# Weights at other distances from the rows they meet, and down slots sorted by row length, in a two-block transformer kernel

## What is computed

```python
def swiglu(x, w_gate, w_up, w_down):                       # D_FF = 2816
    return (silu(x @ w_gate) * (x @ w_up)) @ w_down

def first_block(x, ...):
    for l in range(2):
        h = h + 0.5 * swiglu(rmsnorm(h, ffn1_norm[l]), ...)      # feed-forward parts 1 and 3
        z = rmsnorm(h, mix_norm[l]) @ w_in[l]                    # queries, keys, values, pool, three gates
        branches = stack([mla(z), diff_attention(z), pool(z)])   # each @ w_branch
        h = h + sum(sigmoid(z_gate) * branches) @ w_out[l]
        h = h + 0.5 * swiglu(rmsnorm(h, ffn2_norm[l]), ...)      # feed-forward parts 2 and 4
    return rmsnorm(h, final_norm)

def second_block(x, ...):
    proj = rms_norm(x) @ even_w_in      # even layer: stick-breaking attention and an S5 mixer
    x = x + concatenate([o_a, o_b]) @ even_w_out
    proj = rms_norm(x) @ odd_w_in       # odd layer: gated linear attention
    return x + (o * silu(z)) @ odd_w_out
```

## Time and profile before

| | |
|---|---|
| Median of three runs | 1491.08 us (1490.85 to 1492.25) |
| Profiled execution, its own time | 1489.85 us |
| Its span, first to last instruction | 1487.9 us |
| TensorE busy | 1477.5 us (99%), 9684 matmuls |
| VectorE, ScalarE, GpSimd busy | 1161.2 us (78%), 793.4 us (53%), 39.4 us (3%) |
| Weights and inputs read | 258.61 MB, 175 GB/s over the span |

### The profile page before, as it was taken

The page is one execution under the profiler, slowest core; times in us unless marked ns, Lnnn a source line. Parts: engine busy times, 40 slices in busy tenths (PEclk is TensorE's granted clock), DMA queues, the critical chain, the costliest instruction groups (busy, mean ns, idle before and its releaser), DMA issues.

```text
span 1487.9 us, 23067 instructions
## 1 busy us (share of the span) xinstructions
PE 1477.5 (99%) x9684; PEld 1318.9 (89%) x9684; DVE 1161.2 (78%) x1534; ACT 793.4 (53%) x995; POOL 39.4 (3%) x41
## 2 busy tenths in 40 slices
PE   9999999999999999999999999999999999999999
PEld 8888898888988888888889878799999999989978
DVE  7987777687798865988658677879998799766844
ACT  6444455565454443544436566455545645675653
POOL 0000001210000000000001020000000000000000
PEclk9999999999999999999999999999999999999999
DMA  8555545444455545555554544455554454335531
GB/s 287 203 193 198 173 173 184 158 143 169 166 191 191 192 176 198 188 184 194 183 202 139 192 152 160 151 213 206 193 197 177 154 184 145 142 106 188 178 139 57
DMA packets 38967, 261.15 MB, mean 176 GB/s; under 512 B 4688, under 2 KB 5584, under 8 KB 9168
## 3 DMA queue, kind: packets, MB, share of 16 engines
q1 hardware_dynamic: 38000, 258.62, 49.4%
q10 hardware_dynamic: 864, 1.05, 0.2%
HBM read 258.61 MB, written 1.05 MB: 175 GB/s over the span
## 4 chain that ended last, share of the span: by engine, by line
PE 91%; DVE 7%; ACT 1%; issue 1%; DMA 0%; ACTq 0%
PE ps L285 20%; PE ps L222 13%; PE ps L224 13%; PE ps L223 13%; PE ps L292 11%; PE ps L771 8%; PE ps L773 4%; DVE w_low L207 3%; PE ps L310 1%; PE ps L1513 1%; PE ps L312 1%; DVE scratch L2216 1%; PE ps L1504 0%; DMA w_raw<-in_weights 0%; PE ps L1486 0%
## 5 line engine op out<-in xcount | busy, mean ns | idle before, releaser
L207 DVE TENSOR_TENSOR w_low<-w_raw,w_high 128x2048 fp32r<-128x2048 f32 (+2 forms) x244 | 551.6, 2262 | 152.4 <-ACT w_high L201 150.8
L201 ACT ACTIVATE w_high<-w_raw 128x2048 fp32r<-128x2048 f32 (+2 forms) x244 | 459.7, 1885 | 378.7 <-PE ps L292 171.0
L285 PE MATMUL ps<-x,w_high 128*128 128x512 f32 x1328 | 317.1, 391 | 0.0
L285 PEld LDWEIGHTS ps<-x,w_high 128*128 128x128 f32 x1328 | 243.9, 188 | 47.5
L771 PE MATMUL ps<-ffn_hid,w_high 128*128 128x512 f32 x528 | 183.2, 390 | 0.0
L292 PEld LDWEIGHTS ps<-x,w_low 128*128 128x128 f32 x1328 | 170.3, 191 | 6.4
L292 PE MATMUL ps<-x,w_low 128*128 128x256 f32 x1328 | 173.0, 283 | 0.0
L222 PE MATMUL ps<-w_high,x 128*128 128x512 f32 (+1 forms) x448 | 165.5, 369 | 0.0
L224 PE MATMUL ps<-w_high,x 128*128 128x512 f32 (+1 forms) x448 | 161.1, 360 | 0.0
L223 PE MATMUL ps<-w_low,x 128*128 128x512 f32 (+1 forms) x448 | 160.9, 359 | 0.0
L773 PE MATMUL ps<-ffn_hid,w_low 128*128 128x256 f32 x528 | 148.9, 282 | 0.0
(11 more groups left out here) (476 smaller groups left out, 2323.6 us busy)
## 6 DMA issues: line engine op xcount, KB each, us to landing
w_raw<-in_weights SPq DMA_DIRECT2D x231, 1024.0 KB, 4.9
w_raw<-in_weights SPq DMA_DIRECT2D x10, 768.0 KB, 4.6
w_raw<-in_weights SPq DMA_DIRECT2D x5, 512.0 KB, 4.4
even_second_vectors<-in_second SPq DMA_DIRECT2D x1, 1836.0 KB, 7.5
resid<-in_x SPq DMA_DIRECT2D x3, 256.0 KB, 6.1
w_raw<-in_weights ACTq DMA_DIRECT2D x3, 256.0 KB, 7.1
out<-resid SPq DMA_DIRECT2D x3, 256.0 KB, 2.3
table<-in_table SPq DMA_DIRECT2D x1, 737.0 KB, 8.4
```

The costliest lines, as they stand in the source:

```text
L201: act.activation(self.slot(self.wh, n), self.slot(self.raw, n), ACT.Copy).then_inc(self.hi_made, 1)
L207: dve.tensor_tensor(self.slot(self.wl, n), self.slot(self.raw, n), self.slot(self.wh, n).bitcast(F32), ALU.subtract).then_inc(self.lo_made, 1)
L285: pe.matmul(c.bank(bank + i).rearrange("p (a t) -> p a t", a=2), wh[:, k, i * P:(i + 1) * P], c.x[:, :, k, :], start=(k == 0), stop=False, ...
```

## The change

1. `PHASES` is replaced by two tables, `HIGH_AT` and `LOW_AT`, which `slot` uses for the high and the low part of slot n. `below(rows)` is the start that puts the weights `rows` bytes below 128 modulo 512, the place at which now all streamed rows lie.
2. So that they do, `eps` and `quarter` become one tensor of two columns, `rstd` moves up behind the weights, and `half_column` grows from 32 to 40 columns. Nothing else is done with them.
3. In the down slots of feed-forward parts 1 to 3 all long matmuls of one bank pair in a slot come first, then the short ones.

The distances, worked out from the addresses in the two built programs (rows that stream less the stationary tile loaded meanwhile, in bytes):

| Stage | before | after |
|---|---|---|
| Part 1, gate and up: long / short | 0 / 0 | 0 / 32 |
| Part 2, gate and up: long / short | 0 / 0 | 16 / 64 |
| Part 3, gate and up: long / short | 0 / 0 | -32 / 16 |
| Part 4, gate and up: long / short | 0 / 0 | 0 / 32 |
| Down slots of parts 1, 2, 3: long / short | 32 / 32 | 0 / 32, 16 / 64, -32 / 16 |
| Down slots of part 4 (short) | 32 | 32 |
| Mixer 1: short ones / long ones | 32 / 0 | 64 / 64 |
| Mixer 2: short ones / long ones | 32 / 0 | 96 / 32 |
| Even layer: first eight slots / queries, keys / values (long) / output | 32 / -32 / 0 / 32 | 16 / 32 / 128 / -64 |
| Odd layer: first five slots / values, z (long) / output | 32 / 0 / 32 | 48 / 16 / 128 |

The first two slots of a part, and places where a short one is followed by the load for a long one, have mixed values; the table gives the steady ones.

```diff
-MIX_PHASES = [0 if n < S_DV or S_POOL <= n < S_GATE or n >= S_OUT else LINE for n in range(MIX_SLOTS)]
...
-PHASES = ([LINE] * FF_SLOTS + MIX_PHASES + [LINE] * FF_SLOTS) * DEPTH + EVEN_PHASES + ODD_PHASES
+def below(rows):
+
+    return (LINE - rows // 4) % ROOM
...
+def ffn_at(high, low):
+    return [LINE] + [below(high)] * (FF_SLOTS - 1), [LINE] + [below(low)] * (FF_SLOTS - 1)
...
+FIRST, SECOND, THIRD = ffn_at(0, 32), ffn_at(16, 64), ffn_at(-32, 16)
+MIXERS = [mixer_at(64, -64), mixer_at(96, -32)]
...
+HIGH_AT = FIRST[0] + MIXERS[0] + SECOND[0] + THIRD[0] + MIXERS[1] + LAST_HIGH + EVEN_AT + ODD_AT
+LOW_AT = FIRST[1] + MIXERS[0] + SECOND[1] + THIRD[1] + MIXERS[1] + FIRST[1] + EVEN_AT + ODD_AT
+LOW_AT[1] = LINE
...
-        self.eps = sb("eps", [P, 1])
+        self.constants = sb("constants", [P, 2])
+        self.eps, self.quarter = self.constants[:, 0:1], self.constants[:, 1:2]
...
-        at = 0 if w is self.raw else PHASES[n]
+        at = 0 if w is self.raw else (HIGH_AT if w is self.wh else LOW_AT)[n]
...
-            for j in range(SLOT_TILES):
-                p, k = divmod(SLOT_TILES * m + j, FF_TILES)
-                if p == 0 and k % 2 == 0:
-                    pe.wait_ge(*self.hid_low(k // 2 + 1))
-                if p >= 2 and k == 0:
+            for p in range(4):
+                tiles = [(j, SLOT_TILES * m + j - FF_TILES * p) for j in range(SLOT_TILES)
+                         if 0 <= SLOT_TILES * m + j - FF_TILES * p < FF_TILES]
+                if not tiles:
+                    continue
+                if p >= 2 and tiles[0][1] == 0:
                     pe.wait_ge(*self.down_read(p - 1))
...
+                for j, k in tiles:
+                    if p == 0 and k % 2 == 0:
+                        pe.wait_ge(*self.hid_low(k // 2 + 1))
+                    for i in range(2):
...
+                        pe.matmul(c.bank(bank).rearrange("p (a t) -> p a t", a=2), wh[:, j, f], b.hid[:, :, k, :],
+                                  start=(k == 0), stop=False, skip_group_check=True)
+                for j, k in tiles:
+                    for i in range(2):
...
+                        mm = pe.matmul(c.bank(bank, SEQ), wl[:, j, f], b.hid[:, 0, k, :], start=False,
+                                       stop=(k == FF_TILES - 1), skip_group_check=True)
...
-        self.half_column = sb("half_column", [P, 32])
+        self.half_column = sb("half_column", [P, 40])
```

More of the change, by code:

```diff
@@ L81, with mixer_at @@
 LINE, ROOM = 8, 128
-MIX_PHASES = [0 if n < S_DV or S_POOL <= n < S_GATE or n >= S_OUT else LINE for n in range(MIX_SLOTS)]
-EVEN_PHASES = [0 if n < A_V else LINE for n in range(EVEN_SLOTS)]
-ODD_PHASES = [0 if n < G_V else LINE for n in range(ODD_SLOTS)]
-PHASES = ([LINE] * FF_SLOTS + MIX_PHASES + [LINE] * FF_SLOTS) * DEPTH + EVEN_PHASES + ODD_PHASES
+def below(rows):
+    return (LINE - rows // 4) % ROOM
+LAST_DOWN = FF_SLOTS - 1
+DOWN = (*range(4, LAST_DOWN, 3), LAST_DOWN)
+def ffn_at(high, low):
+    return [LINE] + [below(high)] * (FF_SLOTS - 1), [LINE] + [below(low)] * (FF_SLOTS - 1)
+def mixer_at(three, wide):
+    return [below(wide) if S_DV <= n < S_POOL or S_GATE <= n < S_OUT else below(three) for n in range(MIX_SLOTS)]
+LAST_HIGH = [0 if n in DOWN else LINE for n in range(FF_SLOTS)]
+FIRST, SECOND, THIRD = ffn_at(0, 32), ffn_at(16, 64), ffn_at(-32, 16)
+MIXERS = [mixer_at(64, -64), mixer_at(96, -32)]
+EVEN_AT = [below(16 if n < A_Q else -32 if n < A_V else -128 if n < A_GLU else 32 if n == A_GLU else -64) for n in range(EVEN_SLOTS)]
+ODD_AT = [below(48 if n < G_V else -16 if n < G_OUT else 128) for n in range(ODD_SLOTS)]
+HIGH_AT = FIRST[0] + MIXERS[0] + SECOND[0] + THIRD[0] + MIXERS[1] + LAST_HIGH + EVEN_AT + ODD_AT
+LOW_AT = FIRST[1] + MIXERS[0] + SECOND[1] + THIRD[1] + MIXERS[1] + FIRST[1] + EVEN_AT + ODD_AT
+LOW_AT[1] = LINE
 N_SLOTS = len(SIZES)
@@ L111, in __init__ @@
         self.tab = sb("table", [P, T_WIDTH])
-        self.eps = sb("eps", [P, 1])
+        self.constants = sb("constants", [P, 2])
+        self.eps, self.quarter = self.constants[:, 0:1], self.constants[:, 1:2]
         self.wh = sb("w_high", [P, RING, SLOT + ROOM], F32R)
         self.wl = sb("w_low", [P, RING, SLOT + ROOM], F32R)
-        self.quarter = sb("quarter", [P, 1])
+        self.rstd = sb("rstd", [P, SEQ + 2])
         self.h = sb("resid", [P, DT, SEQ])
@@ L120, in __init__ @@
         self.rt = sb("rms", [P, SEQ])
-        self.rstd = sb("rstd", [P, SEQ + 2])
         self.dist = sb("distance", [P, 3 * P])
@@ L762, in tensor @@
             pe.wait_ge(c.lo_made, c.made(n))
-            for j in range(SLOT_TILES):
-                p, k = divmod(SLOT_TILES * m + j, FF_TILES)
-                if p == 0 and k % 2 == 0:
-                    pe.wait_ge(*self.hid_low(k // 2 + 1))
-                if p >= 2 and k == 0:
-                    pe.wait_ge(*self.down_read(p - 1))
[L769 to L775, removed]
+            for p in range(4):
[4 more added lines that the diff above has]
+                if p >= 2 and tiles[0][1] == 0:
+                    pe.wait_ge(*self.down_read(p - 1))
+                for j, k in tiles:
+                    if p == 0 and k % 2 == 0:
+                        pe.wait_ge(*self.hid_low(k // 2 + 1))
+                    for i in range(2):
+                        f, bank = slice(i * P, (i + 1) * P), B_DOWN + 2 * (p % 2) + i
+                        pe.matmul(c.bank(bank).rearrange("p (a t) -> p a t", a=2), wh[:, j, f], b.hid[:, :, k, :],
+                                  start=(k == 0), stop=False, skip_group_check=True)
+                for j, k in tiles:
+                    for i in range(2):
+                        f, bank = slice(i * P, (i + 1) * P), B_DOWN + 2 * (p % 2) + i
+                        mm = pe.matmul(c.bank(bank, SEQ), wl[:, j, f], b.hid[:, 0, k, :], start=False,
+                                       stop=(k == FF_TILES - 1), skip_group_check=True)
+                if tiles[-1][1] == FF_TILES - 1 and m < LAST:
                     mm.then_inc(c.done, 1)
```

## The result

The changed kernel takes 1493.53 us (median of 19 runs, 1492.29 to 1495.80), the kernel before, run beside it, 1491.64 (19 runs): a ratio of 1.0013, 95% interval 1.0007 to 1.0019. It is slower by about 1.9 us, inside the range of the prediction and on the other side of its forecast, which was 1.6 us faster.

A forecast was written before the change was run, and what follows sets the result against it. The prediction took the pitch of TensorE's 9684 matmuls to bound the kernel. Its terms, -3.5 + 1.3 + 2.5 - 1.4 + 0 - 0.5, summed to -1.6 us, giving about 1489.5 us, with a range of 1474 to 1502.

The forecast's parts named there:

- Short ones of gate and up: Gate and up, all four parts: 1328 short matmuls leaving distance 0 fall from 119.4 to 116.8 ns, -3.5 us.
- Long ones of gate and up: Gate and up, parts 2 and 3: 672 long matmuls moved to 16 and -32 cost 2 ns more each, +1.3 us.
- Long ones of `exact3`: Mixers, even and odd layers: 1260 long matmuls moved from 0 to 64, 32, 128 and 16, +2.5 us.
- Down slots: Parts 1 to 3: 528 alternating pairs become sorted runs, less what 352 long ones off 0 give back, -1.4 us.
- Short ones of `exact3`: Some 2330 short matmuls leave 32, already cheap, for 64, 96, 16, 48, -64 and 128; taken as 0 us.
- Layout and the rest: Merged constants, moved `rstd` and eight extra columns add no instruction, so 0 us.
- 7 us of cover: Down slots, part 1's third slot: VectorE has the hidden rows at 139.8, last wait at 146.9, so TensorE should not stall.
- Same price, +2: Long ones of `exact3` off 0 were charged the same 2 ns over 226.3 as those of gate and up, +2.5 us.
- I take 0: Short ones of `exact3` leaving 32 for other distances: no change forecast, ends -15.8 and +6.1 us.
- The rival on the other side: Long matmuls off 0 become dearer, 230.3 ns; sum +6.7 us, 1498, or 1502 at 232 ns; chance 0.27.
- distance does nothing: Rival: the 2.6 ns belong to the matmul form, pairs stay at 346 to 347 ns, time 1491; chance 0.10.
- Distance helps both lengths: Rival: any distance off 0 takes 2.6 ns off long and short matmuls alike, -12.0 us, 1479; chance 0.25.

The follow-up runs named there:

- e10: Changed kernel with only mixer 2 back at its old distances, short ones 32 and long ones 0; 1490.22 us, ratio 0.9990.
- e1: Changed kernel with every distance put back to before, keeping the new layout and sorted down slots; 1492.13 us, ratio 1.0005.
- e8: Changed kernel with all long matmuls at 0, short ones of `exact3` and of gate and up at 32; 1486.46 us, ratio 0.9971.
- e5: Changed kernel with all long matmuls at 0 and all short ones at -64; 1488.29 us, ratio 0.9979.
- e9: Changed kernel with long ones at 0, short ones of gate and up at 32, of `exact3` at -64 except query and key slots at 32; 1482.15 us, ratio 0.9946.

## Why the prediction was wrong

What bounds the kernel was right: TensorE's pitch. What failed is the sum: -1.6 us forecast, +2.1 measured (the pitches of the two traces subtracted, matmul by matmul, without the first two slots of part 1), +1.9 by the medians. Term by term:

| Term | forecast | measured | what was off |
|---|---|---|---|
| Short ones of gate and up | -3.5 | -3.3 | right: 116.8, 117.8, 117.3 for 32, 64, 16 |
| Long ones of gate and up | +1.3 | +1.4 | right in sum only: 16 gave -0.3, -32 gave +1.4; 0.3 came in parts 1 and 4, still at 0 |
| Long ones of `exact3` | +2.5 | +3.8 | +2 ns taken; +5.2 at 32, +4.8 at 128, +3.7 at 16, +1.4 at 64 |
| Down slots | -1.4 | +0.2 | long ones 229.3 (0) and 232.7 (-32), not 226.3 and 228.3 |
| Short ones of `exact3` | 0 | +1.8 | 96 cost 2.0 us in mixer 2, the odd layer's 48 and 128 0.5; the even layer gave back 0.5 (-1.0 at -64), 64 gave 0.2 |
| Query and key slots | -0.5 | -0.5 | right |
| Layout and the rest | 0 | -1.3 | -0.6 in part 4's down slots, at 32 as before; the rest is spread over transposes, first slots and the edges of runs |

No wait appeared in the down slots, as the 7 us of cover said.

1. **The step that failed is one price for a length.** "Same price, +2" for long ones and "I take 0" for short ones treat every distance off 0 alike. Mixer 2 got the two bad ones, 32 for long ones and 96 for short ones, and it alone is +3.75 us. e10, which puts back these two alone, takes the stage to 216.39 and the whole to 1490.22. The prediction said that it fails if one distance changes the pitch by more than 5 ns; 32 does, by 5.2 on long ones.
2. **The alternating pair was read with its long half too cheap.** From rows 3 the long one at 32 was put at 227.7 to 230.3, by what the short one might cost. In a run it costs 233.3 (e1). In an alternating pair the two together cost 3.4 ns less than apart, so no subtraction in rows 3 could have shown it.
3. **In the down slots the steady 226.3 of rows 5 was used where a run of 16 costs 228.8 in rows 2**, since each has a slow beginning. With 228.8 the term is about 0, as measured. Both rows stood ahead of the prediction.
4. The rival on the other side, dearer long ones, named the right mechanism and the right point: it decides at 2.7 ns on the long ones off 0. They cost 2.5 more in the mean (5.5 us on 2154 pitches), at the edge of that point, and the short ones of `exact3` did the rest. It charged 2.8 us for short ones at 64, -64 and 128; of these only 128 is dear, and the loss came at 96, which it didn't name. That the result lies inside the range is no merit of the sum: the range is 1474 to 1502.
5. The rival "distance does nothing" falls: short ones cost from 113.3 to 120.0 ns in runs, long ones from 227.6 to 235.8 in the mean, and e8, which differs from after in these tables alone and moves no instruction, takes 7.1 us less. With it falls what the prediction drew from the Trainium skill ("SBUF — State Buffer", section "Who interferes with whom"), that with two independent read ports distance is worth nothing. Whether the ports or the memory behind them make the difference, no run here shows.
6. "Distance helps both lengths" falls too: of all distances tried none is more than 2 ns below 0 for long ones.

What stays open: what decides between 113.3 and 117.8 at -64 and 64. The program sets it in most places, as 50 of 56 stretches kept theirs, but not in all. Open is also why the price hangs on the distance at all, and why the clock fell in e5 and not in the profiled execution of e9, where TensorE stood still almost as long at the same place. In other executions e9's clock seems to fall too: two of its five have a mean granted clock of 0.997 and take 1484.67 and 1486.52 us, the others 1481.25 to 1482.15; of e5's eleven, nine have 0.996 to 0.998.

## What to carry to other kernels

Where TensorE is bound by the pitch of its matmuls, measure that pitch for each length and each distance between streamed rows and the weights loaded meanwhile, in runs of one kind, before moving anything; a price from an alternating pair or from one other distance is no price for the one that you will use, and one execution may show only one of two prices. Then keep what pays, by length and stage: here the whole change cost 1.9 us, while two of its distances, 32 in gate and up and -64 in `exact3`, with the long ones left at 0, are worth 8 to 10. A cheaper matmul can also end in a wait for the engine that feeds it, so look at that engine's share in the stage first.

## Unexpected in the hardware

- Beside its columns (106.7 ns for 256 at 2.4 GHz) a short matmul in a run costs 6.6 to 13.3 ns, by the address of its rows against that of the weights loaded meanwhile. The 2.5 ns that the Trainium skill gives for an isolated matmul in "TensorE: Matmul & The Clock Gate", section "Back-to-back issue gap", was reached at no distance here.
- Long and short ones want different distances: 0 is among the best for long ones and almost the worst for short ones.
- One distance can have two prices, 113.3 and 117.8 ns at -64 and at 64, and a stretch holds the one that it has taken; six of 56 stretches of the same program showed the other one in a second execution.
- In e5 a stretch of 1.8 us in which TensorE did next to nothing was followed by 6.8 us at the lower clock level; in the profiled execution of e9 a stop of 2.0 us at the same place was not.
